# Spare products on TensorE, a new order in the second mixer and a new opening, in a two-layer recurrent decoder step

## What is computed

```python
for layer in range(DEPTH):                       # DEPTH = 2
    if layer % 2 == 0:
        mix = even_mixer(x, ...)                 # HGRN2 (4 heads) and GLA (4 heads), w_in: 1024 x 3600
        x = layernorm(ALPHA * x + mix)
        ffn = swiglu(x, w1, w3, w2)              # dense, 2816 hidden
    else:
        mix = odd_mixer(x, ...)                  # mLSTM, 4 heads, dk 128, dv 256, gates, conv of width 4
        x = layernorm(ALPHA * x + mix)
        ffn = moe(x, ...)                        # top 2 of 8 experts, 3584 hidden
    x = layernorm(ALPHA * x + ffn)
```

```python
h = (h - mu) * rsqrt(var + EPS) * hn_w           # mLSTM: per head
y = sigmoid(o_pre) * h
return y @ w_out
# MoE: logits = x @ w_router; the two best experts of each token, softmax of their logits as weights
```

## Time and profile before

| | |
|---|---|
| Time, median of 3 runs | 1592.01 us (1591.88 to 1594.26) |
| The profiled execution's own time | 1594.92 us |
| Its span in the profile | 1592.9 us |
| PE busy | 1521.7 us, 96% |
| DVE busy | 1291.0 us, 81% |
| ACT busy | 1102.5 us, 69% |
| Mean granted TensorE clock | 0.975 |

### The profile page before, as it was taken

One profiled execution on the slowest core, in us unless ns is written; L12 is line 12 of the kernel. 1 busy time (PEld: TensorE's weight loads), 2 busy tenths in 40 slices (PEclk: granted clock), 3 DMA queues, 4 the chain that ended last, 5 costly groups with the idle time before them and its releaser, 6 DMA issues.

```text
span 1592.9 us, 24340 instructions
## 1 busy us (share of the span) xinstructions
PE 1521.7 (96%) x8493; PEld 1315.3 (83%) x8493; DVE 1291.0 (81%) x1591; ACT 1102.5 (69%) x1390; POOL 26.7 (2%) x45
## 2 busy tenths in 40 slices
PE   6999899998899779999999999999999999999996
PEld 6888899998788758888888888888888888888885
DVE  4634666666855768999999999999999999999995
ACT  5435644445645737788788788788788788788884
POOL 0000000000001000000000000000000000000000
PEclk9999999999899979999999999999999999999998
DMA  8432655563534547999999999999999999999991
GB/s 330 155 119 77 185 186 186 211 238 108 213 129 148 192 172 266 371 385 345 377 383 340 376 380 341 376 384 340 376 380 351 373 376 348 374 379 344 381 370 56
DMA packets 54448, 455.01 MB, mean 286 GB/s; under 512 B 6976, under 2 KB 7176, under 8 KB 22128
## 3 DMA queue, kind: packets, MB, share of 16 engines
q1 hardware_dynamic: 47888, 423.74, 69.9%
q0 software_dynamic: 3952, 20.55, 3.7%
q10 hardware_dynamic: 2544, 9.86, 1.6%
HBM read 443.51 MB, written 10.62 MB: 285 GB/s over the span
## 4 chain that ended last, share of the span: by engine, by line
PE 80%; issue 13%; DVE 5%; ACT 1%; DMA 1%; POOL 0%; DVEq 0%; SPq 0%; ACTq 0%; POOLq 0%
PE bank L577 23%; PE bank L578 23%; PE bank L579 23%; PE bank L1207 1%; PE bank L1168 1%; PE bank L572 1%; DVE state L2413 1%; PE bank L696 1%; DVE wlo L1866 1%; DMA ring<-in_w_in 1%; PE bank L604 0%; ACT whi L1305 0%; PE bank L605 0%; PE bank L608 0%; DVE arena L2270 0%
## 5 line engine op out<-in xcount | busy, mean ns | idle before, releaser
L2550 DVE TENSOR_TENSOR wlo<-ring,whi 128x1024 fp32r<-128x1024 f32 x672 | 807.9, 1222 | 55.2 <-ACT whi L1779 13.0
L1779 ACT ACTIVATE whi<-ring 128x1024 fp32r<-128x1024 f32 x672 | 712.3, 1065 | 184.1 <-PE bank L579 182.3
L577 PE MATMUL bank<-whi,high 128*128 128x512 f32 x1344 | 531.7, 396 | 0.0
L579 PE MATMUL bank<-whi,low 128*128 128x512 f32 x1344 | 524.9, 391 | 0.0
L578 PE MATMUL bank<-wlo,high 128*128 128x512 f32 x1344 | 524.3, 390 | 0.0
L579 PEld LDWEIGHTS bank<-whi,low 128*128 128x128 f32 x1344 | 252.8, 188 | 53.6
L577 PE MATMUL bank<-high,whi 128*128 128x264 f32 x936 | 276.0, 295 | 20.8 <-DVE wlo L1866 12.7
L577 PEld LDWEIGHTS bank<-whi,high 128*128 128x128 f32 x1344 | 253.0, 188 | 51.2 <-issue 0.3
L578 PEld LDWEIGHTS bank<-wlo,high 128*128 128x128 f32 x1344 | 253.2, 188 | 50.6
L578 PE MATMUL bank<-low,whi 128*128 128x264 f32 x936 | 270.0, 288 | 0.0
L579 PE MATMUL bank<-high,wlo 128*128 128x264 f32 x936 | 269.6, 288 | 0.0
(11 more groups left out here) (373 smaller groups left out, 1095.5 us busy)
## 6 DMA issues: line engine op xcount, KB each, us to landing
ring<-in_w_moe SPq DMA_DIRECT2D x224, 1536.0 KB, 8.5
ring<-in_w_in SPq DMA_DIRECT2D x25, 1024.0 KB, 5.3
ring<-in_w SPq DMA_DIRECT2D x22, 1024.0 KB, 4.8
ring<-in_w SPq DMA_DIRECT2D x7, 1536.0 KB, 6.6
ring<-in_w_out SPq DMA_DIRECT2D x4, 1536.0 KB, 6.4
state<-in_state ACTq DMA_DIRECT2D x1, 4096.0 KB, 13.3
arena<-vrows POOLq DMA_DIRECT2D x8, 512.0 KB, 5.6
o_Cs<-state POOLq DMA_DIRECT2D x1, 4096.0 KB, 12.2
```

The costliest lines, as they stand in the source:

```text
L577: pe.matmul(out, xh, wh, start=start, stop=False)
L579: return pe.matmul(out, xl, wh, start=False, stop=stop)
L1779: A_(whi[:, g % NSPLIT, :], ring[:, s % RING, (g % 3) * D:(g % 3 + 1) * D], ACT.Copy).then_inc(whi_ready, 1)
L2550: V.tensor_tensor(wlo[:, g % NSPLIT, :], ring[:, s % RING, (g % 3) * D:(g % 3 + 1) * D], whi[:, g % NSPLIT, :].bitcast(F32), ALU.subtract) ...
```

## The change

It has three parts. **Spare products**: TensorE gets rounded products of 264 columns, whose results are not used (the bank is overwritten by the next true product), at seven places: 24 at the very start, on a tile that GpSimd fills with ones; 6 + 5 + 5 ahead of each of the two `projection_by_inputs`; 8 + 3 ahead of the second mixer's output product; 6 + 5 + 5 ahead of the router logits; 10 + 6 ahead of the ranks; 10 + 6 ahead of the gather. Between the groups of one place stands a wait of the chain that PE waits for anyway (`var_ready`, `rstd_ready`, `hstd_ready`, `route1`, the banks). **A new order in the second mixer**: the three exponentials move ahead of a tile's rounding, a convolution tap and a sigmoid on ACT; `state_products(0)` moves behind tile 9 and `key_scores(1)`; at the tail the sample means and variances move forward, the rounding of the last tile moves behind the rounding of `og`, its remainder on DVE behind the `low` parts, and the `low` parts of heads 0 and 1 ahead of head 3's normalisation. **A new opening**: `X` comes in two halves, the first weight tile has a DMA of its own, the constants and `wgr` move from the front (and from ACT's queue) to SP's queue behind the first four tiles, and tile 0 is multiplied first with its `whi` (16 products), then with `wlo` (8).

```diff
@@ TensorE
+            def spin(out, times, stationary, moving):
+                for _ in range(times):
+                    mm = pe.matmul(out, stationary, moving, start=True, stop=True)
+                return mm
...
             def projection_by_inputs(first, last, stage):
                 outs = [job(tiles[g][2])[:, 0:N] for g in range(first, last)]
                 pe.wait_ge(low_ready, last)
+                n = stage - 2
+                spin_on_tile(outs[0], 6, first)
+                pe.wait_ge(var_ready, n + 1)
+                spin_on_tile(outs[0], 5, first)
+                pe.wait_ge(rstd_ready, n + 1)
+                spin_on_tile(outs[0], 5, first)
...
-            projection(0, 1, 0)
-            pe.wait_ge(x_loaded, 32)
+            pe.wait_ge(part_ready, 1)
+            spin_on_tile(bank[0][:, 0:N], 24, NSPLIT - 1).then_inc(spun, 1)
+            out = job(tiles[0][2])[:, 0:N]
+            pe.wait_ge(high_ready, 1)
+            for c in range(KD):
+                pe.wait_ge(xl_ready, c + 1)
...
+            pe.wait_ge(small_loaded, 16 * 8)
             out = job("gr")[0:RANK, 0:N]
...
             def out_projection(first, stage, n):
+                if n == 2:
+                    pe.wait_ge(low_ready, first + 1)
...
+                    spin_on_tile(out, 8, first)
+                    pe.wait_ge(hstd_ready, MH)
+                    spin_on_tile(out, 3, first)
...
             key_scores(0)
+            projection(T + 9, T + 10, 3)
+            key_scores(1)
             pe.wait_ge(state1_loaded, 16)
             pe.wait_ge(qk_ready, max(QK1.index(h) for h in range(MH)) + 1)
             state_products(0)
-            projection(T + 9, T + 10, 3)
-            key_scores(1)
...
+            spare_bank = J[("xt", 0, 0)] % 8
+            wait_bank(spare_bank)
+            spin(bank[spare_bank][:, 0:N], 10, Xh[:, 0, 0:P], Xh[:, 1, :])
             for b in range(8):
                 wait_bank(b)
+            spin(bank[spare_bank][:, 0:N], 6, Xh[:, 0, 0:P], Xh[:, 1, :])
             gather_first()
@@ SyncE
-            sp.dma_start(X[:], A["x"]).then_inc(x_loaded, 16)
-            sp.dma_start(wgr[:], A["w_gr"]).then_inc(x_loaded, 16)
+            for i in range(2):
+                c = slice(KD // 2 * i, KD // 2 * (i + 1))
+                sp.dma_start(X[:, c, :], A["x"][:, c, :]).then_inc(x_loaded[i], 16)
...
+            sp.dma_start(ring[:, 0, 0:D], A["w_in0"][IN0[0]]).then_inc(first_tile_loaded, 16)
+            sp.dma_start(ring[:, 0, D:2 * D], A["w_in0"][IN0[1]]).then_inc(slot_loaded[0], 16)
+            load(1)
+            sp.dma_start(con[:], A["con"]).then_inc(small_loaded, 16)
+            sp.dma_start(vec[:], A["vec"]).then_inc(small_loaded, 16)
+            sp.dma_start(wgr[:], A["w_gr"]).then_inc(small_loaded, 16)
...
-            for s in range(NL):
+            for s in range(2, NL):
@@ ScalarE, head of the second mixer
             take_turned_values1(0)
-            round_tile(TIN1 + 6 + NSPLIT)
-            tap(IN1[6])
-            sigmoid(IN1[4])
             act.wait_ge(lgl_ready, 1)
...
             act.nop().then_inc(exprow_ready, 1)
+            round_tile(TIN1 + 6 + NSPLIT)
+            tap(IN1[6])
+            sigmoid(IN1[4])
@@ ScalarE, tail of the second mixer
-            round_tile(TIN1 + 23 + NSPLIT)
             take_gate1(7)
             head_scale(3)
...
                 round_input(og, 2 * h + 1)
+            round_tile(TIN1 + 23 + NSPLIT)
@@ VectorE, tail of the second mixer
-            tile(23)
             gated1(2)
-            normed1(3)
...
+            for k in range(4):
+                rest_of_input(og, k, 4)
+            normed1(3)
             gated1(3)
             gated_samples1(3)
-            for k in range(2, KD):
+            for k in range(4, KD):
                 rest_of_input(og, k, 4)
+            tile(23)
```

106 lines of the change are left out of this document (66 added, 40 removed), and 4 rows, old and new, of the table behind1.

## The result

The changed kernel took 1574.92 us, the median of four executions (1571.39, 1572.26, 1577.58, 1578.01), against 1593.13 us of the kernel before on the same chip: a ratio of 0.9885, 95% interval 0.9871 to 0.9899. The forecast was 1566.0 with a range of 1558 to 1581. So the gain came, 18.2 us of the 26.5 that were forecast, and the median lies 9 us above the forecast, inside the stated range and outside the forecast's own one of 1560 to 1572. The four executions lie in two pairs, 6 us apart, and that is part of the story. The profiled one is of the faster pair: time 1572.26, span 1570.3.

What follows compares the result with a forecast made beforehand. TensorE, busy 96% of the span, was taken as the bound, shortened only by less waiting or less low-clock work. 4.5 + 3.3 + 4.7 + 3.0 + 0 + 11.0 = 26.5 us off the 1592.0 median gave 1566, range 1558 to 1581.

Steps and rivals of the forecast that it cites:

- signs of being wrong: Clock 0.50 in the gather, `"gr"` waiting beyond 15 us, or new PE waits for ACT or DVE between tiles 10 and 23.
- The opening, 4.5: Program start: with loads reordered, `"gr"` waits for the constants until 13.2 us, before 17.66; PE 4.5 us earlier, bounds 2.5 and 6.
- its worse case: Opening: at a low clock tile 0's 24 products take 5.3 us, end at 13.8, still almost inside the wait for constants.
- The two turns, 3.3: First dense products after two normalisations: 9.2 us each at the high clock, saving 2.1 and 1.2; bounds 0 and 3.9.
- The mixer's head, 4.7: Second mixer's start: value turns begin 5.9 us earlier, minus 1.2 for a low clock at tile 10; bounds 1 and 6.
- the feared fall behind them: Second mixer's head: clock low for tile 10 after the state products, as for tile 9 before; minus 1.2 us.
- The mixer's tail, 3.0: Second mixer's output product: rounding of `og` starts earlier, first output tile done 3.0 us sooner; bounds 1.2 and 4.5.
- Router logits, 0: Spares ahead of the router logits: clock there was already 1.00, so nothing to gain; zero both ways.
- Ranks, gather, first expert, 11.0: High clock saves 1.9 in rank sums, 7.5 gather, 0.7 picks, 2.4 expert, together 12.5; taken as 11, bounds minus 0.7 and 12.5.
- The rival of the slow gather: Gather stays at the low clock; the last term turns from plus 11 to minus 0.7, giving 1577.5 us; chance 0.20.
- The rival that the spares do nothing: Clock falls at every place as before; only opening's order, head and tail gain, giving 1582.8 us; chance 0.07.
- The slower case: Spares stand before ready work at full length, clock low everywhere: 25.3 us against 9.9 gained, giving 1607 us; chance 0.03.

Runs made afterwards that it cites:

- the repeat: The changed kernel again, unedited; 1570.89 us, the median of three executions, with a fourth of 8140 us left out.
- e1: The changed kernel without any of its 115 spare products, new orders and new opening kept; 1580.61 us.
- h4: The changed kernel without the 32 spare products at the two turns, the other 83 kept; 1574.58 us.
- e2: The changed kernel with the second mixer's old order at head and tail on all engines, spares and new opening kept; 1581.29 us.
- h3: The changed kernel with the old order in the second mixer's tail only, the head's new order kept; 1578.47 us.
- g3: The kernel before with only the 32 spare products ahead of ranks and gather added; 1586.03 us against 1593.74.
- h1: The changed kernel with more spares ahead of `"gr"`, the ranks and the first expert, and in six more mixer waits; 1566.55 us.
- e4: The changed kernel without the 32 spare products ahead of the ranks and the gather; 1580.08 us.
- g4: The changed kernel with 25 in place of 5 spares in the last group at both turns and the router logits, 60 more; 1574.60 us.

## Why the prediction was right, and where it was not

The forecast's sum was 26.5 us. The profiles give 22.7, and the medians 18.2, since the profiled execution of before lies above its median and two of the four of after were 6 us slower. None of the prediction's signs of being wrong is in the profile: the clock was 1.00 in the gather, `"gr"` did not wait beyond 15 us, and between tiles 10 and 23 PE has no new wait. By the steps of the prediction:

- **The opening, 4.5.** The arithmetic of landings held: `"gr"` was put at 13.2 and came at 13.39, 4.3 us earlier. But only 2.6 us of it were left at its end, because the clock fell behind the 2.14 us that PE waited for the last constant. The prediction weighed the low clock for tile 0 and left it out for `"gr"`. In the repeat it didn't fall there and 4.4 us were left. Alone, the opening measures 3.5. Its 24 spares have next to no part in that: in e1 tile 0 at the low clock ended inside the wait for the constants, which the prediction had worked out as its worse case.
- **The two turns, 3.3.** Counted as the prediction counts, to the start of the next product, both took 9.60 us where it had 9.2: a gain of 1.8 for 2.1 at the first, 0.8 for 1.2 at the second. (Its upper bound of 3.9 does not follow from its own figures: twice 8.7 against 11.36 and 10.39 gives 4.3.) The clock was 1.00 through both, as forecast. h4's profile has the same size at the two products, 2.5 us, and shows that it need not last: 1.6 us of it are given back before 435 us.
- **The mixer's head, 4.7.** 5.4 us in the milestones. Line 963's wait is gone and the value turns follow `state_products(0)` at once: from its start to theirs it takes 1.0 us, where before took 7.9. But `state_products(0)` did not keep its place, as the prediction had it: it starts 37.9 us after the end of the turn's product, and before it was 36.4. So the 5.4 are 6.9 less 1.5. The state products were put at 1.94 us and took 1.07, since the clock was not low at them, and the feared fall behind them did not come there. It came at tiles 8 and 9, whose 2.6 and 3.6 us of wait for the convolution the prediction did not name.
- **The mixer's tail, 3.0.** 2.3 us by the milestones of before and after, and 2.2 in e2, where it was undone with the head. Undone alone, in h3, it costs 3.8, with more of the clock's low stretches in it. So the forecast was somewhat high.
- **Router logits, 0.** Confirmed: from the logits to the rank sums both profiles need 11.4 to 11.5 us.
- **Ranks, gather, first expert, 11.0.** Here the mechanism was right and the sizes were too high. The ranks gave 1.7 for 1.9. The gather gave 6.5 for 7.5: the prediction halved 15.03, and at a clock of 1.00 it takes 8.49 us, 0.177 us for each of the 48 recorded matmuls, not 0.157. The picks ended no earlier, since the 0.6 us they saved went into a new wait for VectorE, 0.57 us, and the first expert gave 1.1 for 2.4, since the clock fell once more at 576.7 for 3.4 us. Together 9.3 in the profile; alone, in the kernel before, 7.7 (g3).
- **The rival of the slow gather**, 1577.5 at a chance of 0.20, was treated as a property of the kernel. It is one of the execution. With the fast gather the changed kernel takes 1571 to 1572; its other two executions took 1577.6 and 1578.0, which is that rival's number, and their mean clock was 0.982 and 0.984 against 0.989. From the means and the spans, an estimate: some 16 to 22 us more at the low clock. The slow gathers on record come with one low stretch of 20.5 to 27.3 us in place of one of 3.4 (h3, h1, e4), so the size fits. No profile of such an execution of this very kernel exists, so for it the cause is argued; the profiles of h1 and h3 do have the slow gather.

So the step that failed is the choice of 11 for the last term: at its faster executions it should have read 9.3, and two of four had less. The opening's 4.5 stood 1.9 too high for a like reason, a fall of the clock behind a wait that was on the list. The range was drawn to take in the slow gather, and both pairs of executions lie in it. That the median came inside is thus no merit of the sum alone: the sum was 4 us too high by the profiles, and the rest of the distance is the mix of faster and slower executions, on which four of them say little. The rival that the spares do nothing had 1582.8 for its number; e1, where they are left out, measured 1580.61. The slower case priced each spare in the way at its full length, and in g4's profile 20 of them cost 0.4 us and not 2.4.

The prediction drew that price from what the Trainium skill (TensorE: Matmul & The Clock Gate, What overlaps and what doesn't) says, that products start and end in program order. The order held in the rows shown here; the price did not follow at the turns, since the eight inputs behind the spares arrive one by one and a late start only used up the waits between them.

## What to carry to other kernels

A wait on TensorE costs twice where its clock falls behind it, and the second cost can be the larger: 3.5 and 2.1 us of idle ahead of the gather came with 6.5 us more in its products. Cheap products into a free bank, in groups released by the steps of the chain that is waited for, took that away (that groups are needed was not tested), and up to the moment when the real inputs start to arrive they cost nearly nothing; the 32 ahead of the longest stretch of slow work gave more than all the others, and the 24 at the start nothing that any run shows beyond 0.3 us. Price such a change from the place where the slow work is long, expect part of the rest to be given back at the next wait, and time it in enough executions to see whether the times form groups, since a median of four can fall between them.
